# Gate rows of a decoder trunk: built by a matmul instead of a round trip through memory

## The reference

```
ada = cond @ w_ada[layer] + b_ada[layer]
sh_m, sc_m, g_m, sh_f, sc_f, g_f = split(ada, 6)
u = modulate(rmsnorm(h, norm_mix), sh_m, sc_m)
mix = forgetting_attention(u, ...)      # layer 0; nsa_attention in layer 1
h = h + g_m * mix
u = modulate(rmsnorm(h, norm_ffn), sh_f, sc_f)
h = h + g_f * moe_ffn(u, w_router, b_router, experts, shared expert)
```

## Time and profile before

| | us |
|---|---|
| median of 3 executions | 1502.01 (1501.45 to 1502.64) |
| the profiled execution | 1502.64 |
| its span | 1500.9 |
| PE busy | 1409.9 (94%) |
| PEld busy | 808.3 (54%) |
| DVE busy | 313.8 (21%) |
| ACT busy | 261.9 (17%) |
| POOL busy | 36.5 (2%) |

### The profile page before, as it was taken

One profiled execution on the slowest core, in us unless ns is written; L12 is line 12 of the kernel. 1 busy time (PEld: TensorE's weight loads), 2 busy tenths in 40 slices (PEclk: granted clock), 3 DMA queues, 4 the chain that ended last, 5 costly groups with the idle time before them and its releaser, 6 DMA issues.

```text
span 1500.9 us, 20423 instructions
## 1 busy us (share of the span) xinstructions
PE 1409.9 (94%) x8337; PEld 808.3 (54%) x8337; DVE 313.8 (21%) x756; ACT 261.9 (17%) x506; POOL 36.5 (2%) x85
## 2 busy tenths in 40 slices
PE   4999899999999999999879988989999999999997
PEld 1677766645544444444368776764455444444442
DVE  0330512111111111111032576022111111111111
ACT  2211512111111111111123444031111011111110
POOL 4000001000000000000000000010000000000000
PEclk9999999999999999999999979799999999999999
DMA  9999289599999999999998400125999999999996
GB/s 358 421 420 390 96 330 412 240 369 421 421 421 421 421 421 421 421 422 421 420 327 337 147 1 1 56 105 218 388 421 420 422 421 422 421 420 422 420 421 256
DMA packets 72015, 514.42 MB, mean 343 GB/s; under 512 B 8400, under 2 KB 8592, under 8 KB 9968
## 3 DMA queue, kind: packets, MB, share of 16 engines
q1 hardware_dynamic: 70272, 509.64, 83.0%
q0 software_dynamic: 1504, 3.36, 0.8%
q10 hardware_dynamic: 144, 0.08, 0.0%
HBM read 511.98 MB, written 1.06 MB: 342 GB/s over the span
## 4 chain that ended last, share of the span: by engine, by line
PE 80%; DMA 13%; DVE 3%; ACT 2%; issue 1%; SPq 1%; DVEq 0%; ACTq 0%
PE PS L830 19%; PE PS L501 14%; DMA ring<-in_w_exp 11%; PE PS L820 11%; PE PS L838 10%; PE PS L853 10%; PE PS L522 3%; PE PS L881 2%; PE PS L609 2%; DMA ring<-in_w_ada_units 2%; PE PS L484 1%; PE PS L919 1%; PE PS L594 1%; PE PS L427 1%; PE PS L577 1%
## 5 line engine op out<-in xcount | busy, mean ns | idle before, releaser
L830 PE MATMUL PS<-ring,scratch 128*32 128x512 f32 (+2 forms) x2176 | 360.9, 603 | 22.0 <-DMA ring<-in_w_exp 20.3
L830 PEld LDWEIGHTS PS<-ring,scratch 128*32 128x32 f32 (+2 forms) x2176 | 114.1, 124 | 261.9 <-issue 260.0
L820 PEld LDWEIGHTS PS<-scratch,u 128*128 128x128 f32 x1600 | 183.2, 192 | 39.3 <-issue 37.4
L820 PE MATMUL PS<-scratch,u 128*128 128x128 f32 x1600 | 192.4, 278 | 1.4 <-ACT scratch L1037 1.4
L501 PE MATMUL PS<-ring,uT 128*128 128x256 f32 x832 | 185.9, 383 | 1.9 <-ACT u L465 1.1
L838 PE MATMUL PS<-ring,scratch 128*32 128x512 f32 (+2 forms) x1088 | 182.2, 596 | 1.2 <-DVE item_first_i L1154 1.2
L853 PE MATMUL PS<-scratch 128*128 128x512 f32 x400 | 180.1, 593 | 0.0
L501 PEld LDWEIGHTS PS<-ring,uT 128*128 128x128 f32 x832 | 157.5, 191 | 30.6 <-issue 5.9
L1169 DVE TENSOR_TENSOR scratch<-PS,gate_row 128x512 f32<-128x512 f32 x100 | 69.2, 692 | 446.6 <-PE PS L838 446.6
L1045 ACT ACTIVATE scratch<-PS 128x256 f32<-128x256 f32 x50 | 19.2, 384 | 677.5 <-PE PS L830 677.5
L838 PEld LDWEIGHTS PS<-ring,scratch 128*32 128x32 f32 (+2 forms) x1088 | 52.4, 122 | 123.0 <-issue 121.4
(11 more groups left out here) (314 smaller groups left out, 796.5 us busy)
## 6 DMA issues: line engine op xcount, KB each, us to landing
ring<-in_w_exp SPq DMA_DIRECT2D x384, 1024.0 KB, 21.1
ring<-in_w_ada_units SPq DMA_DIRECT2D x56, 1024.0 KB, 13.8
ring<-in_w_in_a_units SPq DMA_DIRECT2D x12, 1024.0 KB, 22.5
ring<-in_w_cmp_units SPq DMA_DIRECT2D x8, 1024.0 KB, 30.8
ring<-in_w_sh_units SPq DMA_DIRECT2D x6, 1024.0 KB, 8.1
ring<-in_w_kv_b_units SPq DMA_DIRECT2D x6, 1024.0 KB, 22.1
ring<-in_w_o_a_units SPq DMA_DIRECT2D x4, 1024.0 KB, 8.0
ring<-in_w_in_b_units SPq DMA_DIRECT2D x4, 1024.0 KB, 12.1
```

Source lines behind the costliest of these rows:

```text
L820: mm = pe_.matmul(PS[:, bank, i * w:(i + 1) * w], u[:, t, k * P:(k + 1) * P], hot[:, t, :], start=(t == 0), stop=(t == NT - 1))
L830: mm = pe_.matmul(PS[places, GU, :], x[:, kk, places], gate_and_up, start=(kk == 0), stop=(kk == KC - 1))
```

## The change

The round trip through memory goes, and with it the tensor `gate_rows`, `write_gate` and `read_gate`. In its place each gate row is made by three engines. VectorE builds `gate_diag` [128, 8, 128] in scratch, the unit matrix times the gate's column k for each k (`dve_gate_diag`). TensorE multiplies it with the matrix of ones in two matmuls of 512 columns (`pe_gate`): the sum over partitions of a diagonal matrix is its diagonal, the same on each of the 128 output rows. ScalarE copies the two PSUM banks to `gate_row` (`act_gate`). The waits on `gate_ready` count 1 for each gate instead of 16, and TensorE waits for it before it turns `u` back into the same banks.

```
@@ build
-        gate_rows = nc.dram_tensor("gate_rows", (4, KC, P), F32, kind="Internal").ap()
+        gate_diag = cut(S0 + 2048, [KC, P])
-        gate_written, gate_ready = sem("gate_written"), sem("gate_row_ready")
+        gate_diag_ready, gate_out, gate_ready = sem("gate_diag_ready"), sem("gate_out"), sem("gate_row_ready")
@@ new functions
+        def dve_gate_diag(done, i):
+            done(done.eng.tensor_tensor(gate_diag, ident[:, :].unsqueeze(1).to_broadcast([P, KC, P]),
+                                        vectors[:, GATES[i], :].unsqueeze(2).to_broadcast([P, KC, P]), ALU.mult),
+                 gate_diag_ready)
+
+        def pe_gate(pe_, i):
+            pe_.wait_ge(gate_diag_ready, i + 1)
+            for half in range(2):
+                mm = pe_.matmul(PS[:, half, :], ones[:, :],
+                                gate_diag[:, 4 * half:4 * half + 4, :].rearrange("p k c -> p (k c)"),
+                                start=True, stop=True)
+            mm.then_inc(gate_out, 1)
+
+        def act_gate(done, i):
+            done.eng.wait_ge(gate_out, i + 1)
+            done(done.eng.activation(gate_row[:, :], PS[:, 0:2, :].rearrange("p b c -> p (b c)"), ACT.Copy),
+                 gate_ready)
@@ pe_moe
             if layer == 0:
                 pe_ada_columns(pe_, 2)
+            pe_gate(pe_, 2 * layer + 1)
             pe_.wait_ge(routing["sigmoids"], layer + 1)
...
+            pe_.wait_ge(gate_ready, 2 * layer + 2)
             for t in range(NT):
                 for k in range(KC):
@@ act_moe
             done(act.activation(narrow_T[E64, :], PS[E64, Y0, 0:SEQ], ACT.Sigmoid), routing["sigmoids"])
+            act_gate(done, 2 * layer + 1)
@@ dve_moe
             dve_modulate(done, tag, OF_LAYER[layer] + SH_F)
+            dve_gate_diag(done, 2 * layer + 1)
@@ GpSimd: write_gate, read_gate and their calls
-            def write_gate(i):
-                pool.dma_start(gate_rows[i].rearrange("k p -> p k"), vectors[:, GATES[i], :],
-                               allow_slow_non_contiguous=True).then_inc(gate_written, 16)
-
-            def read_gate(i, written):
-                pool.wait_ge(gate_written, 16 * written)
-                pool.dma_start(gate_row[:, :], gate_rows[i:i + 1].rearrange("o k p -> o (k p)").partition_broadcast(P)
-                               ).then_inc(gate_ready, 16)
...
@@ TensorE, both output projections (gate 0, and 2 in layer 1)
                 pe_rows_unit(pe_, AT["out_a", j], OUT_BANK[j], uT)
+                if j == 0:
+                    pe_gate(pe_, 0)
@@ ScalarE: act_gate(done, 0) and act_gate(done, 2) directly ahead of act_moe
@@ VectorE, ahead of rope_angles and add_mix (gate 0) and of add_mix (gate 2)
+            dve_gate_diag(done, 0)
```

More of the change, by code:

```diff
@@ L1155, in items @@
                                               in1=item_base_ps, op0=ALU.mult, op1=ALU.add), routing["tables_ready"])
-            dve.wait_ge(gate_ready, 16 * (2 * layer + 2))
+            dve.wait_ge(gate_ready, 2 * layer + 2)
             for g in range(len(GROUPS)):
@@ L1371, in late_loads @@
                 pool.dma_start(w_router, a["w_router_rows"][layer]).then_inc(router_loaded, 16)
-                read_gate(2 * layer + 1, 2 + 2 * layer)
             def gate_shared(layer):
@@ L1377, in gate_shared @@
                 landed(pool, n)
-                pool.wait_ge(gate_ready, 16 * (2 * layer + 2))
+                pool.wait_ge(gate_ready, 2 * layer + 2)
                 for j in range(2):
@@ L1381, in gate_shared @@
                     done(ins, shared_gated if j else None)
[L1383 to L1386, removed]
             late_loads(0)
@@ L1392, in _ @@
                                ).then_inc(nsa_params, 16)
-            write_gate(2)
-            write_gate(3)
-            pool.wait_ge(sem("q_rotated"), 4)
-            read_gate(2, 4)
             late_loads(1)
@@ L1629, in _ @@
                 pe_rows_unit(pe_, AT["out_b", j], OUT_BANK[j], uT)
+                if j == 0:
+                    pe_gate(pe_, 2)
             pe_.wait_ge(mix_added, 8)
@@ L1677, in _ @@
             done(act.activation(cos_t[:, :, :], cos_t[:, :, :], ACT.Sin), sem("rope_ready"))
+            act_gate(done, 0)
             act_moe(done, 0)
@@ L1774, in _ @@
             act_copy_turned(done, uT, "nsa_o")
+            act_gate(done, 2)
             act_moe(done, 1)
@@ L1870, in add_mix @@
             def add_mix(layer, name):
-                dve.wait_ge(gate_ready, 16 * (2 * layer + 1))
+                dve.wait_ge(gate_ready, 2 * layer + 1)
                 for j in range(4):
@@ L2012, in _ @@
             dve_attention(done, "nsa", nsa_batches, nsa_finish, beside_attention)
+            dve_gate_diag(done, 2)
             add_mix(1, "out_b")
```

## The result

| | us |
|---|---|
| after, median of 7 executions | 1511.26 (1505.46 to 1517.58) |
| before, median of 7 | 1502.64 (1498.98 to 1505.26) |
| ratio | 1.0055, 95% interval 1.003 to 1.0082 |
| the profiled execution of after | 1514.47 |
| its span | 1512.7 |

The kernel became slower, by 8.3 us with an interval of 4.5 to 12.3 us (ratio and interval times the time of before).

What follows compares the result with a forecast made beforehand. TensorE's row ahead of each layer's order_i was taken to bound the kernel; the gates' 1.72 + 0.82 + 1.72 + 1.08 = 5.3 us gave 1507.4 us against the median of 1502.01, range 1504.2 to 1510.2.

Steps and rivals of the forecast that it cites:

- What bounds the kernel: Expert loops have fixed length and begin at order_i; each us by which TensorE's row delays it moves the end one us.
- The removal costs and gives nothing: Dropping the gates' writes and reads through memory: value 0, bounds 0 and 7.6 us of gain, 18.6 us of slack.
- relief rival: Freed transfers relieve the stream or layer 0's 2.54 us are absorbed: no change, 1504.8 us (full relief 1499.8); chance 0.09.
- cheap matmul: Rival: each gate matmul is one instruction, a gate 0.86 us, 1.9 us in sum: 1503.9 us, no change; chance 0.03.
- Gates 0 and 2 at 1.72: Behind the output projection's first unit in layers 0 and 1, TensorE's row is full: each gate adds 1.72 us.
- Gate 1 at 0.82: Layer 0, between router and scores' transposes: 0.90 of 1.72 us fall into TensorE's wait for the sigmoid, leaving +0.82.
- Gate 3 at 1.08: Layer 1, between router and scores' transposes: 0.64 of 1.72 us is covered by TensorE's wait, leaving +1.08.
- VectorE, ScalarE and GpSimd hidden: Products, copies and GpSimd's scaling add nothing; the first addition starts 2.9 us later but is caught up by the second unit.
- slow-clock rival: Half clock after layer 1's norm wait reaches over router and gate 3: 3.5 us on top, 1510.9 us; chance 0.08.
- fast-clock rival: The shift prevents the half clock at 933 to 955 us, saving 10.8 us: 1496.6 us; chance 0.05.

Runs made afterwards that it cites:

- router_only: The changed kernel with gates 0 and 2 back on the round trip through memory, gates 1 and 3 by matmul: 1504.81 us, ratio 1.0006 to the kernel before.
- second traces: Both kernels run and traced once more, unaltered: after 1508.33 us, ratio 1.0037; before 1503.97 us, ratio 1.0005.
- after_dense: The changed kernel with four unused matmuls in layer 1's wait for the norm: 1504.15 us, ratio 1.0009 to the kernel before.
- pad_once: The kernel before with two unused matmuls behind the first unit of layer 1's output projection: 1505.79 us in one execution.
- pad_twice: The kernel before with four unused matmuls behind the first unit of layer 1's output projection: 1505.9 us in one execution.
- three_fills: The kernel before with 14 unused matmuls: 6 ahead of layer 1's first norm, 4 around its last heads, 4 in the norm wait: 1490.67 us, ratio 0.9925.

## Why the prediction was right or wrong

**What bounds the kernel: right.** order_i in layer 1 came 10.3 us later in the profiled pair (1035.43 against 1025.17) and SP's wait stayed 22.2 us. What stood ahead of the order moved the end one for one, and the loops kept their length within 1.6 us; 1.2 us of that rest are a longer low clock in the last group.

**The removal costs and gives nothing: right.** Outside the gates, the start and the rows that move with the clock, the stretches are equal to some hundredths of a us, although 2.1 MB of transfers and the tiny writes of the earlier trace rows are gone.

The relief rival falls with it: from order_i to layer 0 added it is -0.24 us, not -2.5. In the second traces it is -1.1 us (470.40 against 471.48), and the last expert group alone is shorter by more than that (5.19 against 6.54 us for the 32 instructions, at a granted clock of 0.70 against 0.55). It is not an earlier transfer: TensorE's wait ahead of them is 3.31 against 3.29 us. Nor did the cheap matmul come, each gate being x4.

**Gates 0 and 2 at 1.72: right**, 1.71 and 1.68. **Gate 1 at 0.82: 0.94. Gate 3 at 1.08: 1.38** (5.49 against 4.11 in router_only, where the router ran at the full clock). Both were taken from the wait of the earlier trace rows less an estimated drain; the group took 1.9 us of slots at gate 3 (L561 at 990.88 to L490 at 992.80 in after_dense), 0.2 more than in a row of equal tiles. The sum of slots is 5.7, 0.4 above the forecast.

**VectorE, ScalarE and GpSimd hidden: right.** The first addition starts at 969.37, 2.9 us behind the unit's end at 966.44, as forecast, the second behind its own unit, the norm no later than TensorE's 1.68. GpSimd scales at 259.80 for 4.78 us and is waited for by no one.

**The failed step is the clock, twice.** The slow-clock rival had the mechanism, "should a low level reach over the router", and priced it at 3.5 us; it came at 1.9, since the level rose before gate 3. I gave it 0.08 because "nothing in the change lengthens that wait". That is true, the bracket reads 4.83 us, and beside the point: the sum put the clock at nothing because no wait grew. The change did not lengthen the wait but moved it, and pad_once and pad_twice show that a move of 1.7 us alone does it. At the end of layer 1 the same kind of thing cost 1.2 us more in both pairs of traces, behind a transfer wait as long as before (3.26 against 3.25 us); no rival had this place. The fast-clock rival was dismissed with the half-truth that the level "followed the kind of work": 22 us from L442 on are indeed low in all traces of both kernels. But with the waits ahead of them filled the same work takes 10.84 us (three_fills), so it followed what TensorE did before.

The second failure is the width. From three runs within 1.19 us I concluded that "no such chance event decides 10 us here", against the Trainium skill (TensorE: Matmul & The Clock Gate, "What's actually happening"), whose rule that the activity monitor runs free of the kernel's start I had quoted. By that rule runs should scatter, and with 34 executions they do, over 18.7 us; the start alone differs by 5.6 us between traces (41.9 to 47.5) of the same instructions there. The router's stretch, by contrast, repeated within 0.02 us in either kernel, so its low clock is no such chance. The measured distances were 8.3 and 5.6 us in two rounds of one and the same pair. The mechanisms found add up to 5.7 + 1.9 = 7.6 us; with the ends of the two expert loops it is 8.9 us in the first pair of traces and 7.7 in the second. Of that the clock, which the forecast put at nothing, is some 3 us in the first pair and 2 in the second, and the slots are 0.4 over the forecast. Both sums lie within the intervals of the two rounds (4.5 to 12.3 and 2.6 to 8.6 us). A range of +2.2 to +8.2 us over the 1502.01 of three runs was too narrow by itself.

**Open:** why a shift of 1.7 us meets a fall and 0 or 3.4 does not is shown by traces, one each for the pads, and not explained. In layer 1's attention, 4.7 us shorter in the second trace of after, the granted clock over 890 to 900 us is 1.00 there and 0.66 in the first; why it was low in one and not in the other was not tried, and neither was the end of the expert loops. Whether a part of the start belongs to the change is open too.

## What to carry to other kernels

A small TensorE job that replaces a transfer costs its full slots when TensorE's row is what the next stage waits for and the transfer had slack: look first who waits for the transfer. Where TensorE waits a few us and then works on the path, look at the clock of what follows; filling the wait with unused matmuls, sized below the wait by their measured price, gave more here (11 us) than the whole change cost (8.3 and 5.6 us). Take the spread of a kernel from tens of executions and not from three.

## What was not expected of the hardware

- How long TensorE's clock stays low behind a wait of 4.8 us depends on a shift of 1.7 us, and repeats: the router took 5.22 to 5.28 us in four traces at that shift, and 3.64 in the ten others (six of them with the wait filled).
- Seven unused matmuls (6.1 us of slots) around three short waits went with a shortening of 19.2 us of nearly continuous TensorE work to 10.84; four (3.5 us) did it as well. Both of these runs had a fill ahead of layer 1's first norm too.
- The last 32 gate and up instructions of an expert loop, behind a wait of 3.3 us for a transfer, took 3.6 to 6.6 us: in layer 1 6.54 and 6.55 in the two traces of after, 5.34 in both of before.
- The same instructions at the start took 41.9 to 47.5 us to the first projection in kernels without a fill there.
- With a ScalarE copy ahead of the wait for the router, the sigmoid's 1.28 us table load came behind that wait and no longer ahead of it.
